# A decoder layer step on one NeuronCore: sample tokens of the RWKV head pairs in compact form, joined with the chain of chunk states, and TensorE's loop over the second expert table written out

## The reference

```python
def _wkv_step(S, inp):
    r, w, k, v, kk, kka = inp
    sa = jnp.einsum('bhij,bhj->bhi', S, -kk)
    S = S * w[:, :, None, :] + sa[..., None] * kka[:, :, None, :] + v[..., None] * k[:, :, None, :]
    y = jnp.einsum('bhij,bhj->bhi', S, r)
    return S, y
```

## Time and profile before

| | |
|---|---|
| median of 3 runs | 4362.78 us (4361.63 to 4368.57) |
| the profiled execution | 4369.68 us; its span 4368.1 us |
| mean granted TensorE clock | 0.937 of full speed |
| busy in the span | PE 3960.5 us, DVE 3024.6 us, POOL 1473.3 us, ACT 1459.7 us |
| instructions | 72112 |

### The profile page before, as it was taken

How to read it: one execution, slowest core, us unless ns; L and a number is a source line. 1 busy time by engine, 2 the same in 40 slices (tenths; PEclk the granted TensorE clock), 3 DMA queues, 4 the chain that set the end, 5 groups by cost and what they waited for, 6 DMA issues and landing times. The chain is left out here.

```text
span 4368.1 us, 72112 instructions
## 1 busy us (share of the span) xinstructions
PE 3960.5 (91%) x29289; PEld 3760.7 (86%) x29289; DVE 3024.6 (69%) x3965; ACT 1459.7 (33%) x2056; POOL 1473.3 (34%) x778
## 2 busy tenths in 40 slices
PE   4897899899989687979999999999988999999997
PEld 3896787788778577969999999999988999999996
DVE  1565454555455533348996888888768999999996
ACT  1343321222122111142223444444424444444333
POOL 0332322332332120003365444444443444444441
PEclk7998998999899678989999999999999999999998
DMA  8221222222222124222248999999989999999994
GB/s 371 83 90 52 80 77 93 82 96 77 83 91 86 47 71 171 77 81 78 93 158 319 388 372 382 384 381 368 385 342 356 377 380 387 382 380 377 365 357 176
DMA packets 214273, 982.33 MB, mean 225 GB/s; under 512 B 21952, under 2 KB 101952, under 8 KB 106560
## 3 DMA queue, kind: packets, MB, share of 16 engines
q1 hardware_dynamic: 92256, 524.19, 31.5%
q0 software_dynamic: 57984, 409.37, 23.9%
q10 hardware_dynamic: 63840, 46.15, 3.2%
HBM read 917.54 MB, written 62.09 MB: 224 GB/s over the span
## 5 line engine op out<-in xcount | busy, mean ns | idle before, releaser
L93 PE MATMUL PS<-first_HH,tail_WH 128*128 128x352 f32 (+1 forms) x3072 | 976.7, 318 | 55.8 <-DVE first_HL L1746 31.7
L95 PE MATMUL PS<-first_HH,tail_WL 128*128 128x352 f32 (+1 forms) x3072 | 960.7, 313 | 0.0
L94 PE MATMUL PS<-first_HL,tail_WH 128*128 128x352 f32 (+1 forms) x3072 | 958.6, 312 | 0.0
L93 PE MATMUL PS<-dn_BH,tail_WH 128*128 128x352 f32 x2048 | 669.6, 327 | 34.4 <-DVE dn_BL L2326 23.9
L95 PE MATMUL PS<-dn_BH,tail_WL 128*128 128x352 f32 x2048 | 661.4, 323 | 0.0
L94 PE MATMUL PS<-dn_BL,tail_WH 128*128 128x352 f32 x2048 | 659.6, 322 | 0.0
L93 PEld LDWEIGHTS PS<-first_HH,tail_WH 128*128 128x128 f32 x3072 | 584.8, 190 | 60.6 <-issue 32.0
L2302 POOL DMA_INDIRECT dn_VR<-in_v_rows,tail_EI x192 | 436.3, 2273 | 573.6 <-DVEq L2345 552.2
L2051 POOL DMA_INDIRECT up_UR<-in_u_rows,tail_EI x192 | 420.1, 2188 | 505.2 <-DVEq L2132 485.7
L94 PEld LDWEIGHTS PS<-first_HL,tail_WH 128*128 128x128 f32 x3072 | 585.2, 190 | 0.5
L95 PEld LDWEIGHTS PS<-first_HH,tail_WL 128*128 128x128 f32 x3072 | 584.6, 190 | 0.0
(11 more groups left out here) (401 smaller groups left out, 7462.0 us busy)
## 6 DMA issues: line engine op xcount, KB each, us to landing
tail_WR<-in_peer_u SPq DMA_DIRECT2D x128, 1024.0 KB, 9.1
tail_WR<-in_peer_v SPq DMA_DIRECT2D x128, 1024.0 KB, 8.3
mix_RING<-in_w_ada SPq DMA_DIRECT2D x88, 1024.0 KB, 4.9
mix_RING<-in_w_in SPq DMA_DIRECT2D x37, 1024.0 KB, 4.8
tmp_z<-up_ZB ACTq DMA_DIRECT2D x128, 176.0 KB, 8.0
tmp_gd<-up_STG ACTq DMA_DIRECT2D x22, 1024.0 KB, 18.3
dn_GG<-tmp_gd SPq DMA_DIRECT2D x16, 1408.0 KB, 10.3
dn_ZI<-tmp_z SPq DMA_DIRECT2D x128, 176.0 KB, 6.3
```

The costliest lines, as they stand in the source:

```text
L93: nc.tensor.matmul(out, r32(wh), r32(xh), start=first, stop=False)
L94: nc.tensor.matmul(out, r32(wh), r32(xl), start=False, stop=False)
L95: return nc.tensor.matmul(out, r32(wl), r32(xh), start=False, stop=last)
```

## The change

The sample tokens leave the chunk form. `SLT` becomes [128, 7, 32] (ST = 32), the steps are two (LEVELS = 5, 5), and the samples are done in `pe_samples`, `act_samples`, `dve_samples` and a part of POOL's `pair`, among the links of step 1's chain. The 32 tokens of all samples form one small system per head (masks MASK4, SEL8), solved by three multiplications (`pe_solve`, `dve_solve`); the new states are the old ones scaled by POOL (SO) plus one product of 64 rows (BKT by UVM). The first half of the projection of pair i+2 is cut in eighths, one behind each link; tile 6 of the modulation lies behind links 0 and 1, tile 7 behind links 4 and 5. Modulation group 2 gets PSUM bank 5, the variances banks 0 and 1. POOL waits for the end of the write of `wkv_p` later. In `phase_down`, PE's loop over the row groups is a Python loop: its instructions are written out. (`u = 3 * i + step` becomes `u = 2 * i + step` throughout, and the branches for step 2 go.)

```diff
-    LEVELS = (5, 5, 2)
+    MOD_BANKS = (6, 6, 5)
+    LEVELS = (5, 5)
-    SLT = m.sb("SLT", [P, 7, 2 * P])
+    SLT = m.sb("SLT", [P, 7, ST])
+    UVM = PREP[0:2 * ST, 8 * P:16 * P].rearrange("p (b v) -> p b v", v=P)
...
+        def pe_solve(pe, i, n):
+            if n == 0:
+                pe.wait_ge(asr_ready, i + 1)
+                pe.wait_ge(m4_ready, i + 1)
+                pe.wait_ge(uv_ready, i + 1)
+                for h in range(2):
+                    at = slice(64 * h, 64 * h + 64)
+                    nc.tensor.matmul(PS[0:ST, 3, at], ASR[:, 0, :], IDENT[:, at], start=True, stop=False)
+                    mm = nc.tensor.matmul(PS[0:ST, 3, at], M4[ST:2 * ST, h, 0, :], UV[ST:2 * ST, at], start=False, stop=True)
+            else:
+                pe.wait_ge(u_ready, 4 * i + n)
+                for h in range(2):
+                    at = slice(64 * h, 64 * h + 64)
+                    mm = nc.tensor.matmul(PS[0:ST, 3, P + 64 * h:P + 64 * h + 64], M4[0:ST, h, 0, :],
+                                          (BB if n == 1 else UV)[0:ST, at], start=True, stop=True)
+            mm.then_inc(u_done, 1)
         def pe_samples(pe, i, ahead2):
-            if ahead2:
-                pe.wait_ge(mod_read, 3 * i + 3)
-                project(pe, i + 2, 0, (0,))
-            pe.wait_ge(gk_ready, u + 1)
-            pe.wait_ge(y0_ready, 2 * u + 2)
+            pe.wait_ge(y0_ready, 4 * i + 4)
             pe.wait_ge(si_in, 32 * i + 32)
+            for b in range(NB):
+                mm = nc.tensor.matmul(PS[:, 4, 2 * NS * b:2 * NS * b + 2 * NS], SI[:, b, :],
+                                      SLT[:, KA_:KR_ + 1, NS * b:NS * b + NS], start=True, stop=True)
+            mm.then_inc(sa_done, 1)
+            pe_turn(pe, i, 1)
+            pe.wait_ge(gk_read, 2 * i + 2)
+            for h in range(2):
+                rows = slice(64 * h, 64 * h + 64)
+                mm = nc.tensor.matmul(PS[0:2 * ST, h, 0:2 * ST], SLT[rows, KB_:KK_ + 1, :].rearrange("p k t -> p (k t)"),
+                                      SLT[rows, KA_:KR_ + 1, :].rearrange("p k t -> p (k t)"), start=True, stop=True)
+            mm.then_inc(sm_prod, 1)
+            nc.tensor.matmul(PS[0:2 * ST, 2, 0:P], SLT[:, KBH:KKH + 1, :].rearrange("p k t -> p (k t)"), IDENT[:],
+                             start=True, stop=True)
+            nc.tensor.matmul(PS[ST:2 * ST, 2, P:2 * P], SLT[:, KV_, :], IDENT[:], start=True, stop=True).then_inc(st_done, 1)
+            pe.wait_ge(gk_ready, 2 * i + 2)
+            pe.wait_ge(mod_read, 3 * i + 2)
             for n in range(8):
-                nc.tensor.matmul(PS[:, 4 + n // 4, P * (n % 4):P * (n % 4) + P], GS[:, n, :], SI[:, n, :],
-                                 start=True, stop=True)
-                mm = nc.tensor.matmul(PS[:, 7, CH_CHUNK * n:CH_CHUNK * n + CH_CHUNK], SI[:, n, :],
-                                      R2[:, n // 4, 32 * (n % 4):32 * (n % 4) + 32], start=True, stop=True)
+                pe_scan(pe, i, 1, n)
+                if n < 4:
+                    pe_solve(pe, i, n)
+                if n in (0, 1):
+                    pe_modulation(pe, i, 6, 8 * n, 8 * n + 8)
+                if n in (4, 5):
+                    pe_modulation(pe, i, 7, 8 * n - 32, 8 * n - 24)
+                if n == 4:
+                    pe.wait_ge(u_ready, 4 * i + 4)
+                    ...
+                        mm = nc.tensor.matmul(PS[rows, 4, 2 * ST:3 * ST], UV[:, rows], M4[:, h, 1, :], start=True, stop=True)
+                    mm.then_inc(ys_done, 1)
+                if n == 5:
+                    pe.wait_ge(um_ready, i + 1)
+                    pe.wait_ge(vm_ready, i + 1)
+                    for half in range(2):
+                        mm = nc.tensor.matmul(PS[:, 2 + half, :], BKT[:], UVM[:, 4 * half:4 * half + 4, :], start=True,
+                                              stop=True)
+                    mm.then_inc(so_prod, 1)
+                if ahead2:
+                    project_half(pe, i + 2, 0, 0, 2 * n, 2 * n + 2)
+            pe_turn(pe, i, 2)
...
+        def act_samples(act, i):
+            A(ASR[:].rearrange("p k (b s) -> p k b s", s=NS),
+              PS[:, 4, 0:2 * ST].rearrange("p (b k s) -> p k b s", k=2, s=NS), ACT.Copy).then_inc(asr_ready, 1)
+            A(BKT[:], PS[0:2 * ST, 2, 0:P], ACT.Copy)
+            A(UV[ST:2 * ST, :], PS[ST:2 * ST, 2, P:2 * P], ACT.Copy).then_inc(uv_ready, 1)
+            act_rows_of(act, i, 2)
...
+                G.tensor_tensor(SO[:], SI[:], bcast(PI[:, PC0 + NS:PC1:NS + 1], 2, P), ALU.mult)
+                pool.wait_ge(uv_ready, i + 1)
+                G.tensor_tensor(UVM[ST:2 * ST], bcast(UV[ST:2 * ST, :], 1, NB), bcast(SEL8[ST:2 * ST, :], 2, P),
+                                ALU.mult)
...
+        def dve_solve(dve, i, n):
+            dve.wait_ge(u_done, 4 * i + n + 1)
+            if n == 0:
+                V.tensor_copy(BB[:], PS[0:ST, 3, 0:P])
+            else:
+                V.tensor_tensor(UV[0:ST, :], PS[0:ST, 3, P:2 * P], BB[:], ALU.add)
+            dve.drain().then_inc(u_ready, 1)
+            if n == 3:
+                V.tensor_tensor(UVM[0:ST], bcast(UV[0:ST, :], 1, NB), bcast(SEL8[0:ST, :], 2, P),
+                                ALU.mult).then_inc(um_ready, 1)
         def dve_samples(dve, i):
+            dve_modulation(dve, i, 1)
+            dve.wait_ge(sm_prod, i + 1)
+            V.tensor_tensor(M4[:], PS[0:2 * ST, 0:2, 0:2 * ST].rearrange("p h (k t) -> p h k t", k=2),
+                            bcast(MASK4[:], 1, 2), ALU.mult).then_inc(m4_ready, 1)
+            V.tensor_copy(SB[:, 0, :], SB[:, 8, :])
+            dve.drain().then_inc(s_ready, 1)
+            for n in range(8):
+                dve_scan(dve, i, 1, n)
+                if n < 4:
+                    dve_solve(dve, i, n)
+                if n == 5:
+                    V.tensor_tensor(YT[:, SEQ:T], ASR[:, 1, :], PS[:, 4, 2 * ST:3 * ST], ALU.add).then_inc(yt_ready, 1)
+            dve.drain().then_inc(sp_ready, 1)
+            V.tensor_tensor(YT[:, 256:SEQ], Y0[:].rearrange("p x t -> p (x t)"), PS[:, 7, 0:256], ALU.add)
+            dve.drain().then_inc(yt_ready, 1)
+            dve_modulation(dve, i, 2)
+            V.tensor_tensor(SO[:].rearrange("p (x c) t -> p x c t", x=2), SO[:].rearrange("p (x c) t -> p x c t", x=2),
+                            PS[:, 2:4, :].rearrange("p x (c t) -> p x c t", c=4), ALU.add)
...
-            with pe.Fori(0, NG // 2) as gi:
+            for gi in range(NG // 2):
                 for par in range(2):
                     for c in range(8):
                         v_tile(gi, par, c)
```

More of the change, by code:

```diff
@@ L778, in chan_view @@
     def chan_view(kind, x, step):
[L780 to L783, removed]
+        lo = 1 + 2 * P * step + P * x
+        return CHN[:, kind, lo:lo + P]
     def two_kinds(rows, kind, x, step):
[L786 to L789, removed]
+        lo = 1 + 2 * P * step + P * x
+        return CHN[rows, kind:kind + 2, lo:lo + P]
     with nc.Block() as block:
@@ L851, in home, with project_half, project @@
             return 1 if isinstance(i, int) and i == 0 else which
[L853 to L863, removed]
+        def project_half(pe, i, which, half, first=0, end=KT):
+            if half == 0 and first == 0:
+                pe.wait_ge(wl_ready, 3 * i + which - 1)
+            cols = slice(TPH * half, TPH * half + TPH)
+            for kt in range(first, end):
+                rows = slice(P * kt, P * kt + P)
+                mm = product(nc, PS[:, BANKS[which] + half, 0:TPH], HIGH[home(i, which)][:, rows],
+                             LOW[home(i, which)][:, rows], HH[:, kt, cols], HL[:, kt, cols], kt == 0, kt == KT - 1)
+            if half == 1 and end == KT:
                 mm.then_inc(slot_used, 1)
                 pe.drain().then_inc(proj_done, 1)
+        def project(pe, i, which):
+            for half in range(2):
+                project_half(pe, i, which, half)
         def project_low(pe, i):
@@ L955, in pe_step @@
         def pe_step(pe, i, step):
-            u = 3 * i + step
+            u = 2 * i + step
             if step:
@@ L1006, in pe_step @@
                     pe_scan(pe, i, step - 1, 2 * lv - 2)
[L1007 to L1014, removed]
+                if lv == 3 or (lv == 1 and step == 0):
                     pe_modulation(pe, i, 3 * step + lv // 2)
@@ L1026, in pe_step @@
                 if step:
-                    pe_scan(pe, i, step - 1, 3 if step == 2 else 2 * lv - 1)
-            if step < 2:
-                pe_modulation(pe, i, 3 * step + 2)
+                    pe_scan(pe, i, step - 1, 2 * lv - 1)
+            pe_modulation(pe, i, 3 * step + 2)
             for x in range(2):
@@ L1048, in pe_step @@
                 mm.then_inc(ry_done, 1)
[L1049 to L1053, removed]
             for x in range(2):
@@ L1120, in pair @@
                 pe.wait_ge(prep_ready, i + 1)
-                for step in range(3):
+                for step in range(2):
```

(6 more changed lines are left out.)

126 lines of the change are left out of this document (62 added, 64 removed).

## The result

The changed kernel takes 4305.4 us, median of 4 runs (4295.2 to 4306.96); the kernel before takes 4365.24 beside it, median of 4 (4361.63 to 4368.57). The ratio is 0.9858 with the interval 0.984 to 0.9876: 60 us faster. The forecast was 4235 us, a gain of 128, with the range 4190 to 4272. So the direction was right and the size was not; the result lies 33 us outside the range.

What follows compares the result with a forecast made beforehand. PE, busy 91% of the span, bounds the kernel, its middle stretch a sparse chain at half clock. Gains of 90.6 (pairs 0 to 5), 36 (pairs 6 and 7), 1 (start) and 0 (loop) gave 4235 us, range 4190 to 4272.

Steps and rivals of the forecast that it cites:

- Part 1: New middle stretch of pairs 0 to 5: 23.8 us where it was 41.3, a gain of 17.5 us a pair.
- the first link: In the middle stretch, the chain's first link starts 4.5 us in.
- links 0 and 1 with tile 6: In the middle stretch, these links up to the end of modulation tile 6 take 3.4 us at full clock.
- The wait for tile 7: In the middle stretch, PE newly waits about 1.0 us for the load of modulation tile 7.
- Pairs 6 and 7: Middle stretch of the last two pairs, without projection as cover: 23 us, a gain of 18 each, 36 us together.
- Part 2: After the head means, POOL's later subtraction delays DVE's row mixing: PE waits 2.4 us a pair, bounds 0 and 5.
- The first collision: After the head means, DVE's row mixing meets POOL's subtraction: DVE's chain loses 4.3 us at the start.
- Part 3: Second table's loop written out: nothing to save at the loop's head, 0 us, bounds 4 lost and 21 gained.
- rival 2: Heads' part: half clock lasts as before, DVE's chain loses the full 5 us; gain 92 us, 4270 us; chance 0.17.
- Rival 4: Second table: written-out instructions come too late, deciding above 3.0 us per added packet; 4403 us at 4 us each; chance 0.04.
- Rival 1: Middle stretches: PE keeps its full clock because the projection's eighths fill the chain; gain 155 us, 4208 us; chance 0.20.

Runs made afterwards that it cites:

- e9: The changed kernel again, unedited, a third time: 4310.39 us, ratio 0.9883 to the kernel before.
- e3: The changed kernel with twelve unread products added in the sparse opening of the middle stretch, pairs 0 to 5: 4270.52 us, ratio 0.9772.
- e7: The changed kernel with e3's products in all eight pairs, six more behind each link in pairs 6 and 7, hardware loop back behind 44 small products: 4251.49 us.
- e2: The kernel before with only the loop of the second table written out: 4383.02 us, ratio 1.0022.
- e6: The kernel before with 45 small unread products ahead of the second table's loop: 4403.2 us, ratio 1.0083.
- e1: The changed kernel with the hardware loop of the second table put back: 4362.22 us, ratio 0.9993 to the kernel before.
- e5: e1 with 19 small unread products (76 instructions) ahead of the loop: 4296.86 us, ratio 0.9835 to the kernel before.
- e4: The changed kernel with the half projection in quarters behind links 0 to 3 instead of eighths behind all, no work added: 4274.51 us, ratio 0.9808.
- e8: The changed kernel with twelve unread products behind the last turn, just ahead of the head means, pairs 0 to 5: 4298.98 us, ratio 0.9843.

## Why the prediction was wrong

**The clock of Part 1, the step that failed most.** I wrote that the new stretch "is sparse for 4.5 us and then filled up like them, so I take 7 us at half clock", at 3.2 us a pair. The measured share at half clock is 7 us in the best pair (2) and 27 in pair 1. The filling was counted as dense work by its busy time; but the clock didn't return until 22 us into pair 0's stretch, although PE was busy 98% of it. The unedited program needs 23.5 us at a clock of 0.93 (e9), so six pairs would take 141 us or less, and they took 179.1. That is 38 us or more for the clock, over 6 a pair and so outside my bounds of 0 to 6, where 19 were set aside: 19 or more of the 36.7 us that these pairs fell short. I had also tied the half clock to the sparse opening; in pair 0 the opening has full clock and the filled part behind it the half one.

**The work of Part 1** was priced too low as well, 20.65 us at full clock, where e9 shows 23.5 at 0.93. e3's pair 0, at 1.00, takes 23.5, or 22.5 without the 1.0 us that its added products put ahead of the first link. L1117 took 1.98 us, outside my bounds of 0.9 to 1.6 and not 1.3: the multiplication of 272 columns by a square weight was the wrong row for it. In e3's pair 0 links 0 and 1 with tile 6 take 4.6 us (568.73 to 573.29) and not 3.4, the first solve alone 0.88 for 0.45. The wait for tile 7 was 1.48 in pair 2, but 0.25 to 0.57 in those of the same pairs 0 to 5 that had a clock of 1.00 (e3, e7), where 1.0 was taken. The first link (4.2 us against 4.5) was right.

**Pairs 6 and 7**: 25.7 and 25.8 us against 23; the clock again (e7: 23.7 and 24.5 with products in the gaps).

**Part 2** held. POOL's subtraction meets the row mixing and DVE's chain is late for the next step 0; the loss was 0.9 to 3.7 us a pair, 1.65 in the mean, against 2.4 taken. The first collision costs 3.3 us and not 4.3. The second subtraction, said to meet the last of the row mixing and the scan, meets L1522 again, which takes 3.40 us where L1457 took 4.76. What I left out is what may follow from the new wait: in two pairs PE enters step 0 at half clock, and steps 0 and 1 grow by 12.1 us over the eight pairs. In e7, where the middle is dense, PE waits as long ahead of step 0 (1.6 to 2.1 us), but L970 takes 1.06 us in pairs 1 to 5, and 9.9 of the 12.1 are gone. So the clock has a part in it. How large a part isn't shown, for these steps take 525.5 us in the kernel before, but 529.4 and 532.3 in e2 and e6, whose heads' part is the same.

**Part 3, the second step that failed.** "There is nothing at the loop's head to save" was read correctly from the row of before, and is false of the changed kernel. Part 1 takes instructions out of PE's stream ahead of the loop and so moves the loop to a place where each return costs 9 us. Beside that loop the writing out saves 49 us; beside the loop of before it costs 10 (e2). So the change's two parts don't add up: Part 1 alone is e1, whose gain can't be told from none. The bounds of 4 us lost and 21 gained were both too narrow, and the forecast for the written-out form itself (0) missed by 11 us. (The row for the first turn also left out its first 30 products, and 14.2 us with them.) The second table, 1014.2 us in the kernel before and 1017.3 in e5, takes 1021.0 in e2, 1021.7 in e4, 1025.5 to 1031.9 in the changed kernel's profiles and e8, and 1038.8 in e3. Waits in turns 2 to 8 (line waited for, us in total, times, longest), first of the kernel before, then of the changed one:

```profile
ACT tail_WH L2257 <- DMA tail_WR<-in_peer_v: 135.7, 34, 7.4
PE PS L93 <- DVE tail_WL L2313: 8.9, 12, 2.8
...
ACT tail_WH L2329 <- DMA tail_WR<-in_peer_v: 157.9, 43, 8.1
PE PS L94 <- DVE tail_WL L2385: 19.1, 20, 2.5
```

These turns are 9.5 us longer, and PE waits 10.2 us more for DVE's subtraction; in e3 they are 23 us longer, with 28.2 us of such waits. ACT waits for the loads of the table for 122 to 136 us in the three kernels whose loop fits (before, e5, e7), and for 158 to 183 in those that are written out. So, as far as the waits show, it is not PE's stream that stalls: the tiles come later. Whether the 42 packets in these turns, of 49 in all (48 were foreseen), are what delays the loads isn't settled.

**The rivals.** Nearest was rival 2, the half clock lasting as long as before (4270), and it was still too mild: by the clock of each middle stretch, the eight are at 1.2 GHz for 129 us before and for 149 in the changed kernel. Rival 4 named the second table and was right in direction against the loop of before, but its price of 3.0 us a packet stands against 11 us for 42 packets; and it missed that fetching can stall a loop more than code written out. Rival 1 (full clock, 4208) was what e3 and e7 go towards.

## What to carry to other kernels

When work leaves TensorE, price what is left at the clock that it will be granted: a stretch of small products can stay at half clock while PE counts as busy, and a dozen dense products in front, or the same work in another order, can bring nearly as much again as the removal (43 us in e3, beside the 60 of the change). A hardware loop whose body is nearly as large as what the engine keeps of its instructions (the size is inferred, the effect measured) depends on where it begins; any edit ahead of it can cost some microseconds per turn. So look at the instruction queue in turns after the first, and at the products at the return, again in the changed kernel, and run each part of a change alone, in both surroundings.

## What was not expected of the hardware

- Added work made a kernel faster: twelve unread products of 276 columns per pair gained 43 us (4270.52 against 4313.18), by keeping the clock at 2.4 GHz.
- The same PE program of 206 instructions took 23.5 to 35.0 us from pair to pair and run to run, by when the clock came back. What decides this in a given pair is open.
- Of a loop of 768 products, seven returns cost nothing (before, e5) or 61.8 us of standing still (e1), with nothing changed but 76 instructions ahead of it. The second table is 59.6 us longer for it.
- After such a stop PE is at half clock as well (0.29 us between products for 0.16). That this makes a stop dearer than its length isn't shown in e1; e6's second table is 33.5 us longer than that of before, with 25 us of stops.
